# A decoder trunk on one core: output projection and feed-forward in one block, the norm's factor applied behind the gate and up products

## The chip, the cores and the metric

The kernel runs on one core of a Trainium2 chip. The metric is the device time of one execution in microseconds (us), the median of several runs. The core has five engines that run side by side, each with its own queue: TensorE (PE; its weight loads are shown apart as PEld), VectorE (DVE), ScalarE (ACT), GpSimd (POOL) and SyncE (SP), which here only issues DMAs. They wait for each other by semaphores that are written out by hand.

## The reference, cut to what matters

Two layers (one even, one odd) work on 1024 prompt tokens and 32 sample tokens, 1056 in all. Each layer is a mixer and a feed-forward part:

```python
def rmsnorm(x, g):
    xf = x.astype(f32)
    return xf * lax.rsqrt(jnp.mean(xf * xf, -1, keepdims=True) + EPS) * g

def swiglu(h, wg, wu, wd):
    return (jax.nn.silu(h @ wg) * (h @ wu)) @ wd

x = x + concat(mixer outputs) @ w_out        # 1024 x 1024
x = x + swiglu(rmsnorm(x, norm_ffn), w_gate, w_up, w_down)   # FF = 2816
```

The factor `rsqrt(mean(x*x) + EPS)` is one number for each token; the gain `g` is one number for each of the 1024 features.

## The kernel before, in words

**Layout.** Activations lie transposed: a tile of 128 partitions (features) by 1056 columns (tokens), eight such tiles for the 1024 features (KD = 8). `g.xt` is the residual stream x, `g.ht` a scratch of the same shape that holds the mixer's output at first, `g.hh` and `g.hl` the high and low halves of the right operand.

**Matrix products.** Every float32 product of these stages is made of three passes in the fp32r type: each operand is split in a high part (rounded by a copy on ACT) and a low part (the difference, a subtraction on DVE), and `split_passes` (L1709) issues high x high, high x low and low x high, each in three thirds of 352 columns. So one weight tile of 128 x 128 costs nine matmuls, and one output tile (eight weight tiles) 72.

**Output projection**, `stage_project_out` (L1510), a block of its own. ACT and DVE split the mixer's output (L1560 to L1563, L1584). For each of the eight output tiles m, SP loads the weights (L1528), ACT and DVE split them (L1558, L1579), PE makes 72 matmuls into PSUM banks 0 to 2 or 4 to 6 (m even or odd), and DVE adds them into x (L1596). ACT squares the new x (L1610) and DVE adds up the squares (L1618), one tile behind.

**Norm**, `split_norm` (L1623), which is the first part of the block of `stage_ffn` (L1718). Its steps follow one another: PE sums the squares over the partitions with nine small products against a column of ones (L1662); DVE scales and adds EPS (L1678), ACT takes the root (L1651), DVE the reciprocal (L1682), all on a tile of 128 x 9; DVE makes nine diagonal tiles (L1686), and PE multiplies them by ones (L1667), which gives the factor replicated over all partitions in PSUM, 128 x 1056. Then DVE multiplies each of the eight tiles of x by gain and factor (L1694), ACT rounds it into `g.hh` (L1656), and DVE and POOL take the low halves in turn (L1643).

**Feed-forward**, the rest of `stage_ffn`. FF = 2816 is 22 hidden tiles f, two for each of 11 chunks. For each hidden tile PE makes the gate product G(f) in banks 0 to 2 and the up product U(f) in banks 3 to 5 (72 matmuls each), and then half of the down product of the chunk before (four output tiles, 72 matmuls in all, banks 0 to 2 and 3 to 5 in turn). ACT applies Silu to the gate (L1874), DVE multiplies it with the up product (L1917), ACT and DVE split the result (L1878, L1922), and DVE adds each down product into x (L1929). Meanwhile SP loads the next weight tiles, ACT rounds them (L1868) and DVE takes their low parts (L1908). Three chunks stand unrolled ahead of a hardware loop and two behind it.

**Order.** Nothing plans the order: it is that of each engine's own program. On DVE a half chunk reads: low part of the down weights, low part of the next gate weights, join (L1917), low part of the next up weights, low part of the hidden tile, four additions into x. On ACT: round the down weights, Silu, round the next gate and up weights, round the hidden tile. PE waits for the split weights, and for a bank to be read before it writes there again; in the lines quoted here `silu` and `joined` are the counts of Silus and joins done:

```python
                                if c == 1 and half == 1:
                                    pe.wait_ge(added, 3 + n)
                                else:
                                    pe.wait_ge((silu, joined)[n], 2 * c + half)
```

Of the kernel before, what the change touches and what calls it, by code (L numbers as in the profile page):

```python
# [23 lines left out]
P = 128  # L24
D = 1024
# [131 lines left out]
def build_program(nc, ins, outs, const_dram, place, kept):  # L157
    with ExitStack() as whole:
# [37 lines left out]
        with ExitStack() as even:  # L196
# [1313 lines left out]
def stage_project_out(g, weight, tag, reload):  # L1510

    nc = g.nc
    x_in, made, added = (g.sem(f"{tag}_{n}") for n in ("stream", "made", "added"))
    w_in, w_rounded, w_split = g.slot_sems(f"{tag}_weights", 2), g.sem(f"{tag}_w_rounded"), g.sem(f"{tag}_w_split")
    rounded, split = g.sem(f"{tag}_rounded"), g.sem(f"{tag}_split")
    square, add_square, _ = sum_squares(g, f"{tag}n", g.ht[:, SQUARES, :], g.ht[:, TOTAL, :])
    with ExitStack() as st:
        w = g.room(st, f"{tag}_w", [P, 2, KD * P])
        wh = g.room(st, f"{tag}_wh", [P, 2, KD * P], F32R)
        wl = g.room(st, f"{tag}_wl", [P, 2, KD * P], F32R)  # L1520
        block = st.enter_context(nc.Block())

        @block.sync
        def _(sp):
            for m in range(KD):
                if m >= 2:
                    sp.wait_ge(w_split, m - 1)
                sp.dma_start(w[:, m % 2, :].rearrange("p (k n) -> p k n", k=KD),  # L1528
                             weight[:, m * P:(m + 1) * P].rearrange("(k p) n -> p k n", p=P)
                             ).then_inc(w_in[m % 2], 16)  # L1530

        @block.gpsimd
        def _(pool):
            if reload:
                for k in range(KD):
                    pool.dma_start(g.xt[:, k, :], g.xt_spill[:, k, :]).then_inc(x_in, 16)

        @block.tensor
        def _(pe):
            for m in range(KD):  # L1540
                pe.wait_ge(w_split, m + 1)
                if m >= 2:
                    pe.wait_ge(added, m - 1)
                for k in range(KD):
                    if m == 0:
                        pe.wait_ge(split, k + 1)
                    cols = slice(k * P, (k + 1) * P)
                    last = split_passes(g, pe, 4 * (m % 2), wh[:, m % 2, cols], wl[:, m % 2, cols], g.hh[:, k, :],
                                        g.hl[:, k, :], k == 0, k == KD - 1)
                last.then_inc(made, 1)  # L1550

        @block.scalar
        def _(act):
            def high(m):
                act.wait_ge(w_in[m % 2], 16 * (m // 2 + 1))
                if m >= 2:
                    act.wait_ge(made, m - 1)
                act.copy(wh[:, m % 2, :], w[:, m % 2, :]).then_inc(w_rounded, 1)  # L1558

            act.copy(g.hh[:, 0, :], g.ht[:, 0, :]).then_inc(rounded, 1)  # L1560
            high(0)
            for k in range(1, KD):
                act.copy(g.hh[:, k, :], g.ht[:, k, :]).then_inc(rounded, 1)  # L1563
            for m in range(1, KD):
                high(m)
                if m >= 2:
                    if m == 2:
                        act.wait_ge(split, KD)
                    act.wait_ge(added, m - 1)
                    square(act, m - 2)  # L1570
            for m in range(KD - 2, KD):
                act.wait_ge(added, m + 1)
                square(act, m)

        @block.vector
        def _(dve):
            def low(m):
                dve.wait_ge(w_rounded, m + 1)
                dve.tensor_tensor(wl[:, m % 2, :], w[:, m % 2, :], wh[:, m % 2, :].bitcast(F32), ALU.subtract  # L1579
                                  ).then_inc(w_split, 1)  # L1580

            for k in range(KD):
                dve.wait_ge(rounded, k + 1)
                dve.tensor_tensor(g.hl[:, k, :], g.ht[:, k, :], g.hh[:, k, :].bitcast(F32), ALU.subtract  # L1584
                                  ).then_inc(split, 1)
                if k == 0:
                    low(0)
            low(1)
            for m in range(KD):
                dve.wait_ge(made, m + 1)  # L1590
                if reload and m == 0:
                    dve.wait_ge(x_in, 16 * KD)
                if m + 2 < KD:
                    low(m + 2)
                xv = g.xt[:, m, :].rearrange("p (c n) -> p c n", c=3)
                dve.tensor_tensor(xv, g.ps[:, 4 * (m % 2):4 * (m % 2) + 3, 0:THIRD], xv, ALU.add).then_inc(added, 1)  # L1596
                if m >= 1:
                    add_square(dve, m - 1)
            add_square(dve, KD - 1)


# [116 lines left out]
def stage_ffn(g, layer):  # L1718

# [9 lines left out]
    KINDS = "GUD"  # L1729
    raw_in = dict(zip(KINDS, g.slot_sems(f"{tag}_raw_in", 3)))  # L1730
# [3 lines left out]
    silu, joined, hid_high, hid_low, added = (g.sem(f"{tag}_{n}") for n in  # L1734
                                              ("silu", "joined", "hid_high", "hid_low", "added"))
    source = {"G": g.ins["w_gate"][layer], "U": g.ins["w_up"][layer], "D": g.ins["w_down"][layer]}

    with ExitStack() as st:
        inverse = g.room(st, f"{tag}_inverse", [P, TILES])
        n_scalar, n_tensor, n_vector, n_gpsimd, wait_normed = split_norm(  # L1740
            g, 2 + layer, f"{tag}n", g.ht[:, SQUARES, :], g.ht[:, TOTAL, :], inverse[:, :], squares_done=True)
# [26 lines left out]
        def _(sp):  # L1768
# [19 lines left out]
            def chunk(c, par):  # L1788
                if at(c, 0):
                    load("G", 0, True)  # L1790
# [15 lines left out]

            chunks(sp.Fori, chunk)

        @block.tensor
        def _(pe):  # L1810
            def hidden(kind, f, first=False):
# [9 lines left out]
            def down(c, par, half, tail=False):  # L1821
# [4 lines left out]
                for m in range(4):  # L1826
                    if tail or m >= 2:
                        pe.wait_ge(added, 8 * c - 9 + 4 * half + m)
                    else:
                        pe.wait_ge((silu, joined)[m], 2 * c + half + 1)  # L1830
# [984 lines left out]
```

## Time and profile before

| | |
|---|---|
| median of three runs | 3229.15 us (3225.47 to 3239.33) |
| the profiled execution's own time | 3233.79 us |
| its span (first to last instruction) | 3231.7 us |
| PE busy | 2905.4 us (90% of the span) |
| DVE, ACT, POOL busy | 1493.0, 730.5, 314.2 us |
| mean granted PE clock | 0.928 |
| output projection of layer 0 | about 959 to 1061 us of the span |
| feed-forward of layer 0 | about 1061 to 1859 us |
| output projection and feed-forward of layer 1 | about 2316 to 3214 us |

The profile shows one execution. Busy times overlap between engines, and matmuls are pipelined, so that the records of neighbouring matmuls overlap too. A granted clock of 1.00 is 2.4 GHz, 0.50 is 1.2 GHz. In a timeline row the first number is the start in us, the second the length of the merged stretch, and the bracket at its end the idle time before it and what ended it.

### The profile page before, as it was taken

What the parts mean: (1) busy time and instruction counts of PE and PEld (TensorE: products, weight loads), DVE (VectorE), ACT (ScalarE), POOL (GpSimd) and SP (SyncE); (2) the same over time, 40 slices, a digit from 0 to 9 for tenths busy, and PEclk for the clock granted to TensorE, in tenths of its full rate; (3) what the DMA queues carried; (4) which work ended last, traced back from release to release, by engine and by line L of the source; (5) the groups of instructions that cost most, each with busy time, mean ns of one, the idle gap of its engine ahead of it and who ended that gap; (6) DMA issues with size and microseconds to landing.
All of it is one profiled execution on the core that took longest, in us unless ns stands there. A gap on an engine that the chain in (4) does not pass through costs nothing. (4 is left out here: it accounts for less than half of the span.)

```text
span 3231.7 us, 38976 instructions
## 1 busy us (share of the span) xinstructions
PE 2905.4 (90%) x16549; PEld 2663.2 (82%) x16549; DVE 1493.0 (46%) x2021; ACT 730.5 (23%) x1166; POOL 314.2 (10%) x287
## 2 busy tenths in 40 slices
PE   8889996638879899999999979958799999999998
PEld 7757775627539899999999979836599999999997
DVE  4789994678313433322332345248423332332333
ACT  3533330235321311111111032132312111111110
POOL 1022222512130100000000010015001000000000
PEclk9989998858989899999999989957699999999999
DMA  5022223143132121121121021010202111112111
GB/s 163 7 87 90 95 73 125 48 141 106 48 123 66 46 59 40 40 60 40 40 59 40 14 44 47 22 33 1 62 21 65 40 53 46 40 43 57 40 40 67
DMA packets 210737, 188.18 MB, mean 58 GB/s; under 512 B 22843, under 2 KB 164415, under 8 KB 210425
## 3 DMA queue, kind: packets, MB, share of 16 engines
q1 hardware_dynamic: 204033, 164.36, 16.9%
q0 software_dynamic: 6528, 21.23, 2.2%
q8 instruction: 139, 2.28, 0.3%
q14 instruction: 37, 0.30, 0.0%
HBM read 152.25 MB, written 33.50 MB: 57 GB/s over the span
## 5 line engine op out<-in xcount | busy, mean ns | idle before, releaser
L1929 DVE TENSOR_TENSOR xt<-ps,xt 128x1056 f32<-128x1056 f32 x176 | 221.0, 1256 | 205.7 <-PE ps L1713 205.7
L1713 PE MATMUL ps<-ffn_high,f_whG 128*128 128x352 f32 x1056 | 230.0, 326 | 13.2 <-DVE ffn_low L1643 7.8
L1713 PE MATMUL ps<-f_hidh,f_whD 128*128 128x352 f32 x1056 | 229.6, 326 | 9.9 <-DVE f_wlD L1908 9.9
L1713 PE MATMUL ps<-ffn_low,f_whG 128*128 128x352 f32 x1056 | 229.1, 325 | 0.0
L1713 PE MATMUL ps<-f_hidh,f_wlD 128*128 128x352 f32 x1056 | 228.9, 325 | 0.0
L1713 PE MATMUL ps<-ffn_low,f_whU 128*128 128x352 f32 x1056 | 228.7, 324 | 0.0
L1713 PE MATMUL ps<-f_hidl,f_whD 128*128 128x352 f32 x1056 | 228.4, 324 | 0.0
L1713 PE MATMUL ps<-ffn_high,f_whU 128*128 128x352 f32 x1056 | 227.8, 324 | 0.0
L1713 PE MATMUL ps<-ffn_high,f_wlG 128*128 128x352 f32 x1056 | 227.6, 324 | 0.0
L1713 PE MATMUL ps<-ffn_high,f_wlU 128*128 128x352 f32 x1056 | 226.6, 323 | 0.0
L728 PE MATMUL ps<-pe_wh,even_high 128*128 128x512 f32 (+1 forms) x504 | 200.2, 397 | 13.3 <-POOL pe_wl L760 13.3
L730 PE MATMUL ps<-pe_wh,even_low 128*128 128x512 f32 (+1 forms) x504 | 198.9, 395 | 0.0
L729 PE MATMUL ps<-pe_wl,even_high 128*128 128x512 f32 (+1 forms) x504 | 198.3, 394 | 0.0
L1713 PEld LDWEIGHTS ps<-ffn_high,f_whG 128*128 128x128 f32 x1056 | 180.3, 190 | 15.5 <-issue 13.2
L1713 PEld LDWEIGHTS ps<-f_hidh,f_whD 128*128 128x128 f32 x1056 | 181.2, 190 | 11.1 <-DVE f_wlD L1908 11.1
L1713 PEld LDWEIGHTS ps<-f_hidh,f_wlD 128*128 128x128 f32 x1056 | 181.9, 189 | 0.0
L1713 PEld LDWEIGHTS ps<-ffn_low,f_whG 128*128 128x128 f32 x1056 | 181.1, 189 | 0.0
L1713 PEld LDWEIGHTS ps<-ffn_high,f_wlG 128*128 128x128 f32 x1056 | 180.9, 189 | 0.0
L1713 PEld LDWEIGHTS ps<-f_hidl,f_whD 128*128 128x128 f32 x1056 | 180.7, 189 | 0.0
L1713 PEld LDWEIGHTS ps<-ffn_high,f_wlU 128*128 128x128 f32 x1056 | 180.5, 189 | 0.0
L1713 PEld LDWEIGHTS ps<-ffn_low,f_whU 128*128 128x128 f32 x1056 | 179.6, 187 | 0.0
L1713 PEld LDWEIGHTS ps<-ffn_high,f_whU 128*128 128x128 f32 x1056 | 179.4, 188 | 0.0
(538 smaller groups left out, 4837.5 us busy)
## 6 DMA issues: line engine op xcount, KB each, us to landing
pe_w<-in_w_in_even_dram SPq DMA_DIRECT2D x7, 2048.0 KB, 8.3
proj<-pe_out SPq DMA_DIRECT2D x56, 256.0 KB, 2.0
ht_even<-in_w_gate_dram SPq DMA_DIRECT2D x22, 512.0 KB, 5.1
ht_even<-in_w_up_dram SPq DMA_DIRECT2D x22, 512.0 KB, 6.3
ht_even<-in_w_down_dram SPq DMA_DIRECT2D x22, 512.0 KB, 3.9
ht_odd<-in_w_gate_dram SPq DMA_DIRECT2D x22, 512.0 KB, 5.1
ht_odd<-in_w_up_dram SPq DMA_DIRECT2D x22, 512.0 KB, 6.3
ht_odd<-in_w_down_dram SPq DMA_DIRECT2D x22, 512.0 KB, 3.9
```

Of the source, the lines that this page charges most:

```text
L728: pe.matmul(to, high, wh[:, m % 2, k, :], start=(k == 0), stop=False)
L729: pe.matmul(to, high, wl[:, m % 2, k, :], start=False, stop=False)
L730: last = pe.matmul(to, low, wh[:, m % 2, k, :], start=False, stop=(k == KD - 1))
L1713: last = pe.matmul(g.ps[0:out_rows, b0 + c, 0:THIRD], lhs, rhs[:, c * THIRD:(c + 1) * THIRD], start=(first and n == 0), stop=(final and n ...
L1929: dve.tensor_tensor(xv, g.ps[:, 3 * (m % 2):3 * (m % 2) + 3, 0:THIRD], xv, ALU.add).then_inc(added, 1)
```

## The change

The two blocks of a layer become one, `stage_mix_out`, and `split_norm` is no longer used there (the odd layer's input stage still has it).

- PE goes from the last output tile of the projection straight to G(0). Of the last output tile, each of the eight weight tiles counts up a semaphore `used`, and as soon as a tile of `g.hh` and `g.hl` has been used for the last time, ACT and DVE overwrite it with the high and low parts of gain times x (`high_x`, `low_x`), with no factor in it.
- The squares now lie in two slots (there were four). Behind G(0), PE multiplies the summed squares by an all-ones 128 x 128 tile: three float32 matmuls, two of 512 columns and one of 32 (`replicate`), into banks 6, 7 and the free end of bank 2. DVE takes mean and EPS from PSUM into an SBUF tile of 128 x 1056 in three pieces, ACT takes the root of that tile, DVE its reciprocal.
- In each of the 22 hidden tiles, DVE multiplies the gate product by the factor (`scale`, PSUM to SBUF), ACT applies Silu to that SBUF tile in place, and DVE multiplies the result once more by the factor (`regate`), so that the join with the unscaled up product is right. PE's wait for banks 0 to 2 is now for `scaled`.
- DVE's order in a half chunk is now: low part of the down weights, `scale`, `regate`, low part of the next gate weights, join, and so on. ACT's Silu waits for `scaled` instead of the gate product.
- POOL has no part in the low halves any more. The projection's split weights lie in the room of the hidden tiles, and the first gate, up and down weights are loaded, and the gate and up weights split, while the projection still runs.

```diff
 def build_program(nc, ins, outs, const_dram, place, kept):
...
-            stage_project_out(g, ins["w_out_even"][0], "oe", reload=True)
-            stage_ffn(g, 0)
+            stage_mix_out(g, ins["w_out_even"][0], 0, reload=True)
...
-            stage_project_out(g, ins["w_out_odd"][0], "oo", reload=False)
-            stage_ffn(g, 1)
+            stage_mix_out(g, ins["w_out_odd"][0], 1, reload=False)
...
-def stage_ffn(g, layer):
+def stage_mix_out(g, weight, layer, reload):
...
+    total, inverse = g.ht[:, 7, :], g.ht[:, 5, :]
+    square, add_square, squares_added = sum_squares(g, f"{tag}n", g.ht[:, 3:5, :], total)
...
+        out_wh, out_wl = (x[:, :, :, :].rearrange("p a b n -> p (a b n)")[:, 0:2 * KD * P]
+                          .rearrange("p (s n) -> p s n", s=2) for x in (hidh, hidl))
         gate, prod = g.ht[:, 3, :], g.ht[:, 4, :]
+        spreads = ((0, 6, 0, 512), (512, 7, 0, 512), (SEQ, 2, THIRD, NS))
+        gain = g.gain[:, 2 + layer, :]
...
         def _(pe):
+            def mix(m):
+                pe.wait_ge(w_split, m + 1)
+                if m >= 2:
+                    pe.wait_ge(joined_x, m - 1)
+                for k in range(KD):
+                    if m == 0:
+                        pe.wait_ge(mix_split, k + 1)
+                    cols = slice(k * P, (k + 1) * P)
+                    last = split_passes(g, pe, 4 * (m % 2), out_wh[:, m % 2, cols], out_wl[:, m % 2, cols],
+                                        g.hh[:, k, :], g.hl[:, k, :], k == 0, k == KD - 1)
+                    if m == KD - 1:
+                        last.then_inc(used, 1)
+                if m < KD - 1:
+                    last.then_inc(made_out, 1)
+
+            def replicate():
+
+                pe.wait_ge(squares_added, KD)
+                for t0, bank, to, n in spreads:
+                    last = pe.matmul(g.ps[:, bank, to:to + n], g.c("ones"), total[:, t0:t0 + n], start=True, stop=True)
+                last.then_inc(spread_out, 1)
+
             def hidden(kind, f, first=False):
                 pe.wait_ge(split[kind], f + 1)
                 for k in range(KD):
                     if first:
-                        wait_normed(pe, k)
+                        pe.wait_ge(x_split, k + 1)
...
-                                    pe.wait_ge((silu, joined)[n], 2 * c + half)
+                                    pe.wait_ge((scaled, joined)[n], 2 * c + half)
+                            else:
+                                pe.wait_ge(joined_x, KD - 1 + n)
...
                         hidden(kind, 2 * c + half, first=at(c, 0) and half == 0 and n == 0)
+                        if at(c, 0) and half == 0 and n == 0:
+                            replicate()
...
         def _(act):
+            def high_x(k):
+                act.wait_ge(used, k + 1)
+                act.wait_ge(joined_x, k + 1)
+                act.activation(g.hh[:, k, :], g.xt[:, k, :], ACT.Copy, scale=gain[:, k:k + 1]).then_inc(x_rounded, 1)
...
-            def activate(f, first=False):
-                act.wait_ge(made["G"], f + 1)
-                if not first:
-                    act.wait_ge(joined, f)
-                act.activation(thirds(gate), g.ps[:, 0:3, 0:THIRD], ACT.Silu).then_inc(silu, 1)
+            def activate(f):
+                act.wait_ge(scaled, f + 1)
+                act.activation(gate, gate, ACT.Silu).then_inc(silu, 1)
...
             high("G", 0, True)
             high("U", 0, True)
-            n_scalar[1](act)
+            for k in range(KD):
+                if k in (0, KD - 1):
+                    act.wait_ge(joined_x, KD - 1 if k == 0 else KD)
+                    square(act, KD - 2 if k == 0 else KD - 1)
+                high_x(k)
+            act.wait_ge(mean_ready, 1)
+            act.activation(inverse, inverse, ACT.Sqrt).then_inc(root_ready, 1)
             chunks(act.Fori, chunk)
...
         def _(dve):
...
+            def low_x(k):
+                dve.wait_ge(x_rounded, k + 1)
+                dve.scalar_tensor_tensor(out=g.hl[:, k, :], in0=g.xt[:, k, :], scalar=gain[:, k:k + 1],
+                                         in1=g.hh[:, k, :].bitcast(F32), op0=ALU.mult, op1=ALU.subtract
+                                         ).then_inc(x_split, 1)
...
+            def scale(f):
+                dve.wait_ge(made["G"], f + 1)
+                dve.tensor_tensor(thirds(gate), g.ps[:, 0:3, 0:THIRD], thirds(inverse), ALU.mult).then_inc(scaled, 1)
+
+            def regate(f):
+                dve.wait_ge(silu, f + 1)
+                dve.tensor_tensor(gate, gate, inverse, ALU.mult).then_inc(gated, 1)
+
             def join(f, first=False):
-                dve.wait_ge(silu, f + 1)
+                dve.wait_ge(gated, f + 1)
...
                 if not at(c, 0):
                     low("D", 2 * c - 2)
+                scale(2 * c)
+                regate(2 * c)
                 low("G", 2 * c + 1)
                 join(2 * c, first=at(c, 0))
...
-            n_vector[0](dve)
...
+            for m in range(KD - 1):
+                join_x(m)
+                if m >= 1:
+                    add_square(dve, m - 1)
             low("G", 0)
             low("U", 0)
-            n_vector[1](dve)
+            add_square(dve, KD - 2)
+            for k in range(KD - 1):
+                low_x(k)
+            join_x(KD - 1)
+            low_x(KD - 1)
+            add_square(dve, KD - 1)
+            dve.wait_ge(spread_out, 1)
+            for t0, bank, to, n in spreads:
+                last = dve.tensor_scalar(inverse[:, t0:t0 + n], g.ps[:, bank, to:to + n], 1.0 / D, EPS, ALU.mult, ALU.add)
+            last.then_inc(mean_ready, 1)
+            dve.wait_ge(root_ready, 1)
+            dve.reciprocal(inverse, inverse).then_inc(inverse_ready, 1)
+            dve.wait_ge(inverse_ready, 1)
             chunks(dve.Fori, chunk)
```

`join_x(m)` is the former addition into x (L1590 to L1596) under another name; for the last tile it waits for `used` to reach eight.

## Rows read from the trace of the kernel before

**Rows 1.** The page, part 1: busy time of each engine.

```profile
PE 2905.4 (90%) x16549; PEld 2663.2 (82%) x16549; DVE 1493.0 (46%) x2021; ACT 730.5 (23%) x1166; POOL 314.2 (10%) x287
```

**Rows 2.** Busy time by stretch: length, PE, PEld, DVE, ACT, POOL, PEclk, DMA share, GB/s.

```profile
1300.00:1500.00 200.00, 199.16 (x1236) 198.87 (x1235) 58.53 (x49) 28.85 (x28) 0.00 (x0) 1.00 0.17 48
1050.00:1060.00 10.00, 10.00 (x64) 10.00 (x63) 1.40 (x2) 1.09 (x1) 0.00 (x0) 1.00 0.00 0
1100.00:1110.00 10.00, 10.00 (x64) 10.00 (x63) 3.65 (x3) 2.13 (x2) 0.00 (x0) 1.00 0.18 53
```

**Rows 3.** Timeline of PE between the projection and U(0), layer 0.

```profile
1064.74 3.74 PE L1662 MATMUL ps<-cst,ht_even 128*128 128x1 f32 x18 [4.14 <-PEq L1517]
1069.60 4.35 PE L1667 MATMUL ps<-ht_even,cst 128*128 128x128 f32 x18 [1.12 <-DVE ht_even L1686]
1077.84 1.22 PE L1713 MATMUL ps<-ffn_high,f_whG 128*128 128x352 f32 x3 [3.90 <-DVE ffn_low L1643]
...
1082.01 0.65 PE L1713 MATMUL ps<-ffn_high,f_wlG 128*128 128x352 f32 x3
1082.49 0.65 PE L1713 MATMUL ps<-ffn_high,f_whG 128*128 128x352 f32 x3
```

**Rows 4.** Timeline of DVE, layer 0: last two additions of the projection, first join.

```profile
1048.98 1.26 DVE L1596 TENSOR_TENSOR xt<-ps,xt 128x1056 f32<-128x1056 f32 x1 [6.88 <-PE ps L1713]
...
1060.64 1.26 DVE L1596 TENSOR_TENSOR xt<-ps,xt 128x1056 f32<-128x1056 f32 x1 [9.24 <-PE ps L1713]
...
1104.56 1.26 DVE L1917 TENSOR_TENSOR ht_even<-ps,ht_even 128x1056 f32<-128x1056 f32 x1 [8.45 <-PE ps L1713]
```

**Rows 5.** Timeline of DVE, layer 1: last addition of the projection, first join.

```profile
2418.40 1.26 DVE L1596 TENSOR_TENSOR xt<-ps,xt 128x1056 f32<-128x1056 f32 x1 [9.24 <-PE ps L1713]
...
2461.28 1.26 DVE L1917 TENSOR_TENSOR ht_odd<-ps,ht_odd 128x1056 f32<-128x1056 f32 x1 [8.45 <-PE ps L1713]
```

**Rows 6.** Timeline of PE in the sample attention: a run of float32 matmuls.

```profile
939.72 16.47 PE L1449 MATMUL ps<-pages,as_kt 128*128 128x512 f32 x38
```

**Rows 7.** Groups by line and form: xcount | busy us, mean ns | idle before, releaser.

```profile
L590 DVE COPY fr_scale<-ps 128x512 f32<-128x512 f32 x2 | 1.3, 686 | 4.1 <-PE ps L395 4.1
L1694 DVE SCALAR_TENSOR_TENSOR ht_even<-xt,gain,ps 128x1056 f32<-128x1056 f32 x8 | 10.1, 1308 | 0.6 <-PE ps L1667 0.6
L1908 DVE TENSOR_TENSOR f_wlG<-ht_even,f_whG 128x1024 fp32r<-128x1024 f32 x22 | 26.9, 1225 | 229.2 <-ACT f_whG L1868 229.2
L1656 ACT CAST ffn_high<-ht_even 128x1056 fp32r<-128x1056 f32 x8 | 8.6, 1079 | 7.8 <-DVE ht_even L1694 7.3
```

**Rows 8.** Timeline of ACT, layer 0: the table load ahead of the first Silu.

```profile
1088.54 1.28 ACT L1874 ACT_TABLE_LOAD   x1
```

**Rows 9.** Reciprocals, by line: duration in ns as min/median/max.

```profile
L1345 DVE RECIPROCAL at_stat<-at_stat x32: 144/159/164, 747.0 to 840.2; 128x1 f32<-128x1 f32 x32
...
L1682 DVE RECIPROCAL f_inverse<-f_inverse x2: 215/216/217, 1069.0 to 2426.3; 128x9 f32<-128x9 f32 x2
...
L2775 DVE RECIPROCAL sd_rs<-sd_rs x1: 267/267/267, 2303.1 to 2303.1; 128x18 f32<-128x18 f32 x1
...
L1055 DVE RECIPROCAL rt_ms<-rt_ms x1: 379/379/379, 667.8 to 667.8; 128x36 f32<-128x36 f32 x1
```

**Rows 10.** Who waited for whom, layer 0's feed-forward (1110 to 1858 us): total, times, longest.

```profile
PE ps L1713 <- DVE f_wlD L1908: 5.0, 2, 2.5
```

**Rows 11.** Busy time by stretch, columns as in rows 2: six us from each such stall's end.

```profile
1828.00:1834.00 6.00, 5.16 (x22) 5.16 (x23) 1.19 (x2) 0.00 (x0) 0.00 (x0) 0.72 0.28 87
1844.00:1850.00 6.00, 5.22 (x23) 5.23 (x24) 1.35 (x2) 0.00 (x0) 0.00 (x0) 0.72 0.00 0
3186.00:3192.00 6.00, 6.00 (x27) 6.00 (x28) 1.26 (x1) 0.00 (x0) 0.00 (x0) 0.72 0.25 87
3202.00:3208.00 6.00, 6.00 (x38) 6.00 (x39) 1.26 (x1) 0.00 (x0) 0.00 (x0) 1.00 0.01 3
```

More of the change, by code:

```diff
@@ L1507, in _ @@
                                     [list(turned_out.ap[0]), [P + NT, H], [H * NT, NB], [1, NT]]))
[L1510 to L1599, printed above, removed]
@@ L1729, in stage_ffn @@
     KINDS = "GUD"
+    x_in, made_out, joined_x = (g.sem(f"{tag}_{n}") for n in ("stream", "made_out", "added_out"))
+    w_in, w_rounded, w_split = g.slot_sems(f"{tag}_weights", 2), g.sem(f"{tag}_w_rounded"), g.sem(f"{tag}_w_split")
+    mix_rounded, mix_split, used = g.sem(f"{tag}_mix_rounded"), g.sem(f"{tag}_mix_split"), g.sem(f"{tag}_used")
+    x_rounded, x_split = g.sem(f"{tag}_x_rounded"), g.sem(f"{tag}_x_split")
+    spread_out, mean_ready, root_ready, inverse_ready = (g.sem(f"{tag}_{n}") for n in
+                                                         ("spread", "mean", "root", "inverse_ready"))
     raw_in = dict(zip(KINDS, g.slot_sems(f"{tag}_raw_in", 3)))
@@ L1805, in chunk, with _ @@
                     load("U", 2 * c + 2)
-            chunks(sp.Fori, chunk)
+            for m in range(KD):
+                if m >= 2:
+                    sp.wait_ge(w_split, m - 1)
+                sp.dma_start(w[:, m % 2, :].rearrange("p (k n) -> p k n", k=KD),
+                             weight[:, m * P:(m + 1) * P].rearrange("(k p) n -> p k n", p=P)
+                             ).then_inc(w_in[m % 2], 16)
+            chunks(sp.Fori, chunk)
+        @block.gpsimd
+        def _(pool):
+            if reload:
+                for k in range(KD):
+                    pool.dma_start(g.xt[:, k, :], g.xt_spill[:, k, :]).then_inc(x_in, 16)
         @block.tensor
         def _(pe):
+            def mix(m):
+                pe.wait_ge(w_split, m + 1)
+                if m >= 2:
+                    pe.wait_ge(joined_x, m - 1)
[14 more added lines that the diff above has]
+                last.then_inc(spread_out, 1)
             def hidden(kind, f, first=False):
@@ L1829, in down @@
                     else:
[L1830 removed]
+                        pe.wait_ge((scaled, joined)[m], 2 * c + half + 1)
                     for k in range(2):
@@ L1883, in chunk @@
                     high("D", 2 * c - 2, first=at(c, 1))
-                activate(2 * c, first=at(c, 0))
+                activate(2 * c)
                 high("G", 2 * c + 1)
@@ L1905, in _, with low_out, join_x @@
         def _(dve):
+            def low_out(m):
+                dve.wait_ge(w_rounded, m + 1)
+                dve.tensor_tensor(out_wl[:, m % 2, :], w[:, m % 2, :], out_wh[:, m % 2, :].bitcast(F32), ALU.subtract
+                                  ).then_inc(w_split, 1)
+            def join_x(m):
+                if m < KD - 1:
+                    dve.wait_ge(made_out, m + 1)
+                else:
+                    dve.wait_ge(used, KD)
+                if reload and m == 0:
+                    dve.wait_ge(x_in, 16 * KD)
+                if m + 2 < KD:
+                    low_out(m + 2)
+                xv = thirds(g.xt[:, m, :])
+                dve.tensor_tensor(xv, g.ps[:, 4 * (m % 2):4 * (m % 2) + 3, 0:THIRD], xv, ALU.add).then_inc(joined_x, 1)
+            def low_x(k):
[3 more added lines that the diff above has]
+                                         ).then_inc(x_split, 1)
             def low(kind, x):
@@ L1942, in chunk @@
                     low("D", 2 * c - 1)
+                scale(2 * c + 1)
+                regate(2 * c + 1)
                 if not final:
```

40 lines of the change are left out of this document (30 added, 10 removed).

## The prediction, made before the changed kernel was run

> **What bounds the kernel now.** I read the page's busy times first: PE is busy for nine tenths of the span, DVE for under half, ACT for a quarter [rows 1]. So only what moves PE's work, or the gaps in it, moves the end. Next the busy times by stretch: inside the feed-forward PE has no gaps to speak of (199.16 of 200 us) at a granted clock of 1.00 [rows 2]. There nothing can be won without fewer matmuls, and the change takes none away. Then the places where PE does stop. The largest in these two stages is the way from the projection to the feed-forward. After the last projection product PE starts the small sums 4.14 us late, for a new block begins; sums and replication take 3.74 and 4.35 us of short products in which the array does little, with 1.12 us between; then it waits 3.90 us for the first split tile; and the gate product starts at 1.22 us for three matmuls against 0.65 later on [rows 3], at half clock. The whole way, from the last addition of the projection, which starts as its last product ends, to the first join, which starts as U(0) ends, takes 1104.56 - 1060.64 = 43.92 us in layer 0 [rows 4] and 2461.28 - 2418.40 = 42.88 us in layer 1 [rows 5]. Of this only G(0) and U(0) are needed.
>
> **A unit.** Three matmuls of 352 columns follow the last three after 1082.49 - 1082.01 = 0.485 us [rows 3] (0.48 as printed; several such steps give 0.485), so a weight tile costs 1.455 us and a product of 72 matmuls 24 x 0.485 = 11.65 us. Times below are us after the last projection product ended.
>
> **The change, part by part.**
>
> *Block boundary, sums, replication and scaling are gone from between the products.* PE can begin G(0) at 0 if the split tiles are there. That has to be followed on DVE. Its addition of output tile 6 starts as the last output tile does, at -11.65 [rows 4]. From there it does that addition, a sum of squares, two weight splits, another sum, seven `low_x` and the last addition: six instructions at up to 1.26 and seven at up to 1.31 us, the price of the like instruction that reads PSUM [rows 4, 7]. That is 16.7 us, so the last addition ends at 5.1. ACT then squares (1.1) and rounds (1.1) tile 7 [rows 7], DVE takes its low half (1.3) and the last sum (1.25): the eighth split tile stands at 8.6, the sum at 9.9. PE wants the eighth tile at 7 x 1.455 = 10.2 and the sum at 11.65. Slack 1.6 and 1.8 us, so I cost `high_x` and `low_x` at nothing; the cover is G(0) itself, and if it were short, each us late would be a us on PE, in each layer. Tiles 0 to 6 are overwritten behind the counts of `used`, one every 1.455 us, and rounding (1.1) keeps up; what sets their time is DVE, and tile 4, the first one made after 0, is ready near 1.3 and wanted at 5.8. POOL's share of the low halves is gone from the path.
>
> *Weights.* SP's queue now passes the first gate, up and down loads behind the eighth projection load, whose slot comes free as output tile 3 ends, four tiles or 46 us before 0; they only wait for the mixer's output to be split, which is older still. DMA share there is near zero [rows 2]. Nothing.
>
> *Replication.* Each float32 matmul shows as two records (the nine sums of L1662 are x18 [rows 3]). With 512 columns a record takes 16.47 / 38 = 0.43 us [rows 6], so two matmuls are 1.73 us, and I give 0.15 to the one of 32 columns: 1.9 us, on the path of PE. It ends at 13.55, and U(0) at 25.2.
>
> *The factor.* Behind the replication: mean and EPS in three pieces from PSUM, two at 0.69 [rows 7] and a short one, 1.5, to 15.0; root on ACT, 1.1 [rows 7], to 16.1. The table load for the root has stood before the wait, and the one for Silu (1.28 [rows 8]) fits while DVE takes the reciprocal. That reciprocal is the unknown: the trace has none beyond 36 columns. From 9 to 36 columns it grows by (379 - 216) / 27 = 6.04 ns a column [rows 9], so 1056 columns make 0.38 + 1020 x 6.04 ns = 6.5 us. The low end is the price of an ordinary instruction of that length, 1.3 us; the high end is twice the slope, 12.8 us, as nothing near this length is shown. I take 6.5: the slope is steady between the rows. It ends at 22.6.
>
> *The Trainium skill on this.* The page "VectorE: DVE Perf Modes", section "First, the fixed hardware budget", says that a reciprocal runs as an iterative divide with a repeat count of 8. If that meant eight cycles for each column at the 0.96 GHz of the quick reference of "Trainium Kernel Development and Optimization", an estimate from the pages would be 8.8 us, 2.3 more in each layer, and the result 3204.5; the slope in rows 9 speaks for less.
>
> *The first hidden tile.* PE reaches G(1) at 25.2. G(1) needs its weights split, and on DVE that split now stands behind `scale` and `regate`. From 22.6: scale 1.26 (23.9), Silu 1.1 (25.0), regate 1.26 (26.2), low part of the gate weights 1.23 (27.5) [rows 4, 7]. ACT's rounding of those weights (1.1) runs beside `regate`. So PE waits 2.3 us and G(1) starts at 27.5, not 25.2. Everything behind it has time: the join and the split of the up weights end near 30, wanted at 39.
>
> *The sum of this.* Layer 0: 43.9 - 27.5 = 16.4. Layer 1: 42.9 - 27.5 = 15.4. Together 31.8 us.
>
> *The clock.* A stall of 2.5 us [rows 10] already stands twice in each layer's last chunk, four in all. In the six us behind it the granted clock was 0.72 on average three times and 1.00 once [rows 11]. 0.72 over six us is 0.28 x 6 = 1.7 us of PE's time. The new stall is nearly as long, one for each layer, so I take off 2 x 0.75 x 1.7 = 2.5 us. Gain 29.3.
>
> *The steady part.* In each of the 44 hidden tiles DVE does two more instructions of 1.26 us and ACT none (Silu reads SBUF instead of PSUM). Queued behind them are the gate weights' split and, later, the join. `scale` starts when G ends; `regate` is done by 3.6, the split by 4.9 after G, and U takes 11.65: DVE is waiting for U again by then, as it is today (8.45 us idle before a join [rows 4]). PE waits for the gate weights only after U and the down product. Banks 0 to 2 come free at the same time as before. Cost nothing; the cover is some 6 us of DVE's idle time under U. SP's next gate load waits for the split and so starts about 2 us later, with over 10 us to spare.
>
> Against the profiled execution (3233.79) this makes 3204.5. That execution was 4.6 us above the median of the runs, 3229.15, so for the median I say **3199.9**.
>
> **Rivals.**
>
> *No stall at G(1).* A reciprocal at the low end would leave the whole chain done by 22.3, before U(0) ends at 25.2. Then 43.9 + 42.9 - 2 x 25.2 = 36.4 us are won and the clock stays: 3192.8. For it: every other long DVE instruction here costs near 1.2 ns a column. Against it: the slope of rows 9.
>
> *A dearer reciprocal.* At twice the slope the stall is 8.6 us, and the gain 31.8 - 12.6 - 3.4 (clock lost both times) = 15.8: 3213.4. For it only that no row is as long; from 9 columns down to 1 the slope is (216 - 159) / 8 = 7.1 ns [rows 9], not much more.
>
> *Slower.* The added DVE work disturbs PE in every hidden tile: 44 x 2.52 = 111 us of added instructions, half of them reading PSUM while PE writes there. If PE ran at half pace under them it would lose 55 us against 29 won: 3229 + 26 = 3255. It decides from 29.3 / 88 = 0.33 us lost for each added instruction. Against it: in ten us with 3.65 us of DVE work PE issues 64 matmuls, as in ten us with 1.40 [rows 2].
>
> *The change does not take the way out.* If the split tiles came late (DVE's list longer than I count, or the squares in two slots holding ACT up), G(0) would start in pieces. Eight us late in each layer would leave 13 us, 3216. The slack of 1.6 us speaks against it, thin as it is.
>
> **How the numbers follow.** The forecast (3195 to 3206, with the reciprocal between 5.5 and 9 us and the clock lost never or twice) gets 0.76, no stall 0.07, a dearer reciprocal 0.08, late tiles 0.05, slower 0.04. The range of 3190 to 3211 holds the forecast, the case without stall and the cheaper half of the dear reciprocals, and some 2 us at each end for the scatter of a median (the runs before lie 14 us apart). A measurement of this kernel can tell about 0.5%, 16 us, from no change: below 3213 counts as faster. Forecast, no stall and most of the dear reciprocals lie there, 0.91; the same 0.05; slower 0.04.
>
> **What would show it.** Right: no idle time on PE between the last projection product and G(0); two pairs of long float32 records behind G(0); a reciprocal near 6.5 us; one gap of 2 to 2.5 us before G(1) that ends on the split of the gate weights; 27.5 us from the last projection product to G(1). In the steady part the join still waits for PE, and PE is busy for over 99%. Wrong: gaps inside G(0) (late tiles), a reciprocal of 1 or 12 us, more than 0.485 us for three matmuls while `scale` runs, or the gate weights' split as a releaser of PE in later chunks.

## The result, and the profile after

| | before | changed |
|---|---|---|
| median | 3231.94 us (8 runs, 3225.47 to 3239.33) | 3213.47 us (8 runs, 3205.95 to 3218.39) |
| profiled execution's own time, span | 3233.79, 3231.7 us | 3209.71, 3207.9 us |
| DVE busy | 1493.0 us | 1602.9 us |

The ratio is 0.9939 (95% interval 0.9928 to 0.9950): faster by 16 to 23 us, 18.5 by the medians. Forecast were 29.3 and a time of 3199.9, in a range of 3190 to 3211. The sign was right, the size was not. Of the 13.6 us between the forecast time and the measured one, 10.8 are missing gain; the other 2.8 are the kernel before, whose median was 3229.15 us in the first three runs and 3231.94 in all eight.

The page's first part and a stretch inside the first feed-forward, which answer to [rows 1, 2] (columns of the second as there):

```profile
PE 2901.5 (90%) x16489; PEld 2659.8 (83%) x16489; DVE 1602.9 (50%) x2083; ACT 734.6 (23%) x1166; POOL 293.4 (9%) x279
```

```profile
1300.00:1500.00 200.00, 198.98 (x1230) 198.69 (x1229) 78.11 (x65) 29.23 (x29) 0.00 (x0) 1.00 0.14 41
```

PE is as busy as before, at the same granted clock, but in the same 200 us it issues 1230 matmuls and not 1236. That is where the largest part of the missing gain is; more below.

**The way from the projection to the feed-forward.** The timeline of PE in layer 0, which answers to [rows 3]:

```profile
1056.65 0.65 PE L1619 MATMUL ps<-ffn_high,f_hidl 128*128 128x352 f32 x3
1057.14 0.65 PE L1619 MATMUL ps<-ffn_high,f_whG 128*128 128x352 f32 x3
...
1068.31 0.65 PE L1619 MATMUL ps<-ffn_high,f_wlG 128*128 128x352 f32 x3
1068.80 2.02 PE L1754 MATMUL ps<-ht_even,cst 128*128 128x512 f32 x6
1070.65 0.73 PE L1619 MATMUL ps<-ffn_high,f_whU 128*128 128x352 f32 x3
...
1085.13 0.72 PE L1619 MATMUL ps<-ffn_high,f_whG 128*128 128x352 f32 x3 [2.59 <-DVE f_wlG L1903]
```

The first row is the end of the last projection product (its split weights now lie in `f_hidh` and `f_hidl`); G(0) follows it with no gap. The float32 product takes 1068.80 to 1070.65, then U(0). The one gap, 2.59 us, ends on the low part of the next gate weights. The timeline of DVE over the same time says why:

```profile
1045.68 1.26 DVE L1893 TENSOR_TENSOR xt<-ps,xt 128x1056 f32<-128x1056 f32 x1 [6.88 <-PE ps L1619]
...
1060.07 1.25 DVE L1893 TENSOR_TENSOR xt<-ps,xt 128x1056 f32<-128x1056 f32 x1
1063.54 1.32 DVE L1897 SCALAR_TENSOR_TENSOR ffn_low<-xt,gain,ffn_high 128x1056 fp32r<-128x1056 f32 x1 [2.22 <-ACT ffn_high L1820]
1064.78 1.25 DVE L1524 TENSOR_TENSOR ht_even<-ht_even 128x1056 f32<-128x1056 f32 x1
1070.85 1.39 DVE L1980 TENSOR_SCALAR ht_even<-ps 128x512 f32<-128x512 f32 x3 [4.82 <-PE ps L1754]
1073.39 6.75 DVE L1983 RECIPROCAL ht_even<-ht_even 128x1056 f32<-128x1056 f32 x1 [1.16 <-ACT ht_even L1871]
1080.18 1.26 DVE L1908 TENSOR_TENSOR ht_even<-ps,ht_even 128x1056 f32<-128x1056 f32 x1
1082.59 1.26 DVE L1912 TENSOR_TENSOR ht_even<-ht_even 128x1056 f32<-128x1056 f32 x1 [1.15 <-ACT ht_even L1830]
1083.77 1.22 DVE L1903 TENSOR_TENSOR f_wlG<-ht_even,f_whG 128x1024 fp32r<-128x1024 f32 x1
```

The last output tile starts at 1045.68, and the last product ends 11.65 us later, at 1057.33. From there the eighth split tile stands at 7.5 us and the last sum at 8.7 (forecast 8.6 and 9.9, wanted at 10.2 and 11.65). Reciprocal, `scale`, Silu, `regate` and the split form one chain, and G(1) starts at 27.8 (forecast 27.5).

The way is measured below to the join of hidden tile 1, behind U(1), so that the loss of clock behind the stall is in it. The rows that give it, for layer 0 and layer 1 (in layer 1 of the changed kernel, output tile 7 starts at 2394.52): first the kernel before, then the changed one:

```profile
1127.79 1.26 DVE L1917 TENSOR_TENSOR ht_even<-ps,ht_even 128x1056 f32<-128x1056 f32 x1 [8.44 <-PE ps L1713]
2484.52 1.26 DVE L1917 TENSOR_TENSOR ht_odd<-ps,ht_odd 128x1056 f32<-128x1056 f32 x1 [8.44 <-PE ps L1713]
```

```profile
1110.30 1.26 DVE L1920 TENSOR_TENSOR ht_even<-ps,ht_even 128x1056 f32<-128x1056 f32 x1 [6.90 <-issue]
2394.52 1.26 DVE L1893 TENSOR_TENSOR xt<-ps,xt 128x1056 f32<-128x1056 f32 x1 [6.88 <-PE ps L1619]
2459.13 1.26 DVE L1920 TENSOR_TENSOR ht_odd<-ps,ht_odd 128x1056 f32<-128x1056 f32 x1 [6.90 <-issue]
```

That is 67.2 and 66.1 us before, 52.95 and 52.95 after.

The busy times of the six us behind that gap, one row for each layer, with the clock as in [rows 11]:

```profile
1085.00:1091.00 6.00, 5.87 (x27) 5.90 (x28) 3.55 (x3) 1.07 (x1) 0.00 (x0) 0.72 0.60 175
2434.00:2440.00 6.00, 6.00 (x28) 6.00 (x29) 3.38 (x3) 1.08 (x1) 0.00 (x0) 0.72 0.60 175
```

The granted clock was at half for part of it in both layers: 0.28 x 6 = 1.7 us each. The four stalls in the last chunks, which [rows 11] shows for the kernel before, are there after the change as well, each of 2.48 us:

```profile
1814.00:1820.00 6.00, 5.51 (x34) 5.51 (x35) 1.69 (x2) 0.00 (x0) 0.00 (x0) 1.00 0.27 87
1828.00:1834.00 6.00, 5.11 (x22) 5.11 (x23) 1.25 (x2) 0.00 (x0) 0.00 (x0) 0.72 0.01 3
3162.00:3168.00 6.00, 5.98 (x37) 5.98 (x38) 1.26 (x1) 0.00 (x0) 0.00 (x0) 1.00 0.27 90
3176.00:3182.00 6.00, 5.58 (x34) 5.58 (x35) 1.63 (x2) 0.00 (x0) 0.00 (x0) 1.00 0.00 0
```

Here the clock fell once in four, before the change three times in four. The stalls are as long as before, so that difference is luck of the two profiled executions.

**The steady part.** Two joins that follow one another in the first feed-forward, from the timelines of DVE, first the kernel before, then the changed one:

```profile
1185.86 1.26 DVE L1917 TENSOR_TENSOR ht_even<-ps,ht_even 128x1056 f32<-128x1056 f32 x1 [8.44 <-PE ps L1713]
1220.67 1.26 DVE L1917 TENSOR_TENSOR ht_even<-ps,ht_even 128x1056 f32<-128x1056 f32 x1 [8.44 <-PE ps L1713]
```

```profile
1203.52 1.26 DVE L1920 TENSOR_TENSOR ht_even<-ps,ht_even 128x1056 f32<-128x1056 f32 x1 [6.90 <-issue]
1238.48 1.26 DVE L1920 TENSOR_TENSOR ht_even<-ps,ht_even 128x1056 f32<-128x1056 f32 x1 [6.90 <-issue]
```

From join to join, three products of 72 matmuls, it takes 34.81 us before and 34.96 after, and this repeats to 0.01 us in most steps. DVE is idle for 6.9 us ahead of the join in either layer, so its queue has not closed up. (The profile names no releaser for that wait; but the join at 1238.48 starts 0.25 us after PE began the product behind U, at 1238.23, so it still waits for PE.) PE itself is slower, by 0.7 ns for each matmul (161.9 for 161.2). With about 40 such steps in the two feed-forwards this is 40 x 0.147 = 5.9 us. Nothing in the forecast had it.

### The profile page after: what moved, and what is told of

It is laid out like the page before. It is cut to its first block and busy times, and to the rows that moved or that the text cites. A ratio compares the mean times of both kernels' runs of the same rounds, so it can differ in the third digit from the quotient of the medians.

```text
span 3207.9 us, 38868 instructions
## 1 busy us (share of the span) xinstructions
PE 2901.5 (90%) x16489; PEld 2659.8 (83%) x16489; DVE 1602.9 (50%) x2083; ACT 734.6 (23%) x1166; POOL 293.4 (9%) x279
```

## The experiments

All times "from the last projection product" are read as above: the start of the addition of output tile 6 plus 11.65 us.

**The pace: addresses or DVE's added work?** The change takes away a tile of 128 x 9 (36 bytes a partition) that lay ahead of the block's other tiles, and adds DVE work under PE. (It also lays the projection's raw weights, two slots of 4096 bytes a partition, ahead of the split ones; e1_offset leaves them there.) Three kernels tell these apart.

```diff
 # e1_offset, on the changed kernel
+        g.room(st, f"{tag}_pad", [P, TILES])
         w = g.room(st, f"{tag}_w", [P, 2, KD * P])
```

> The changed kernel with one unused tile of 128 x 9 (36 bytes a partition) laid out ahead of its own tiles, as the norm's small tile was in the kernel before. The whole computation is done. Theory A (the steady part grew from 34.81 to 34.96 us from join to join because the tiles that PE reads lie at other addresses): 34.81 here, so some 6 us less over the two feed-forwards. Theory B (it grew because DVE now does two more instructions in each hidden tile): 34.96 as in the changed kernel.

```diff
 # e2_before_aligned, on the kernel before: stage_ffn
-        inverse = g.room(st, f"{tag}_inverse", [P, TILES])
...
         hidl = g.room(st, f"{tag}_hidl", [P, 2, 2, T], F32R)
+        inverse = g.room(st, f"{tag}_inverse", [P, TILES])
```

> The kernel before with the small tile of 128 x 9 laid out behind the feed-forward's other tiles instead of ahead of them; nothing else is touched. Theory A (addresses): 34.96 us from join to join instead of 34.81. Theory B (added DVE work): 34.81 as before.

```diff
 # e3_no_scale, on the changed kernel
-                scale(2 * c)
-                regate(2 * c)
...
-                scale(2 * c + 1)
-                regate(2 * c + 1)
...
-                act.activation(gate, gate, ACT.Silu).then_inc(silu, 1)
+                act.activation(thirds(gate), g.ps[:, 0:3, 0:THIRD], ACT.Silu).then_inc(silu, 1)
```

The waits for `scaled` on PE and for `gated` in the join are for `silu` there, as in the kernel before.

> The changed kernel without scale and regate in the hidden tiles: ACT applies Silu straight from PSUM as before, so the factor of the norm is left out of the result; it is still computed. Theory A (addresses): 34.96 us from join to join, as in the changed kernel. Theory B (added DVE work): back to 34.81. Under both the first gate split still stands behind the reciprocal: ready near 24.1 us after the last projection product instead of 27.8, so before U(0) ends at 25.3, and no stall at G(1).

Two joins in a row from the timelines of DVE of e1_offset, of e2_before_aligned and of e3_no_scale, in this order:

```profile
1201.48 1.26 DVE L1921 TENSOR_TENSOR ht_even<-ps,ht_even 128x1056 f32<-128x1056 f32 x1 [6.88 <-issue]
1236.30 1.26 DVE L1921 TENSOR_TENSOR ht_even<-ps,ht_even 128x1056 f32<-128x1056 f32 x1 [6.87 <-issue]
```

```profile
1182.08 1.26 DVE L1917 TENSOR_TENSOR ht_even<-ps,ht_even 128x1056 f32<-128x1056 f32 x1 [8.47 <-PE ps L1713]
1217.04 1.26 DVE L1917 TENSOR_TENSOR ht_even<-ps,ht_even 128x1056 f32<-128x1056 f32 x1 [8.46 <-PE ps L1713]
```

```profile
1197.59 1.26 DVE L1922 TENSOR_TENSOR ht_even<-ps,ht_even 128x1056 f32<-128x1056 f32 x1 [8.47 <-PE ps L1619]
1232.55 1.26 DVE L1922 TENSOR_TENSOR ht_even<-ps,ht_even 128x1056 f32<-128x1056 f32 x1 [8.46 <-PE ps L1619]
```

34.81, 34.96 and 34.96. The unused 36 bytes bring the old pace back under all of DVE's new work, so the raw weights ahead of them are not the cause either; moving the small tile away gives the kernel before the slow pace with none of it; and taking DVE's work out of the changed kernel does not help the pace. All three verdicts go to the addresses. Single times: 3200.76, 3235.62 and 3197.09 us beside 3229.89 for the kernel before on that chip. The first and the third lie some 7 us lower than the traces explain from 3213.47 (one run each, against eight that spread over 12 us), so the pace is read from the profiles.

e3_no_scale also had no stall at G(1), as both theories said: the join of hidden tile 1 starts 48.6 us after the last projection product, where the changed kernel has 52.95.

**The stall at G(1).** e4_early_split does the split of the second gate tile where DVE waits for the root:

```diff
 # ACT
-                high("G", 2 * c + 1)
+                if not at(c, 0):
+                    high("G", 2 * c + 1)
...
+            high("G", 1)
             act.wait_ge(mean_ready, 1)
...
 # DVE
-                low("G", 2 * c + 1)
+                if not at(c, 0):
+                    low("G", 2 * c + 1)
...
             last.then_inc(mean_ready, 1)
+            low("G", 1)
             dve.wait_ge(root_ready, 1)
```

> The changed kernel with the second gate tile's weights rounded on ACT ahead of the root and their low part taken on DVE between the mean and the reciprocal, where DVE waits for ACT. My theory (the stall of 2.59 us at G(1) is the queue position of that split behind scale and regate, and the half clock behind the stall follows from it): the split is ready near 17 us, scale is done near 24.2, U(0) ends at 25.3, no gap at G(1), no half clock behind it: 2.6 + 1.7 us in each layer, 8.6 in all, against the changed kernel. Rival (the stall moves: scale comes late because the split delays the reciprocal, or the clock falls anyway): a gap of over 1 us before G(1) that ends on scale, or a fall of the clock without one, and 0 to 4 us in all.

From its timeline of DVE, and the busy times behind the place where the stall was:

```profile
1071.14 1.39 DVE L1983 TENSOR_SCALAR ht_even<-ps 128x512 f32<-128x512 f32 x3 [4.83 <-PE ps L1754]
1072.45 1.22 DVE L1905 TENSOR_TENSOR f_wlG<-ht_even,f_whG 128x1024 fp32r<-128x1024 f32 x1
1073.68 6.75 DVE L1987 RECIPROCAL ht_even<-ht_even 128x1056 f32<-128x1056 f32 x1
1080.47 1.26 DVE L1910 TENSOR_TENSOR ht_even<-ps,ht_even 128x1056 f32<-128x1056 f32 x1
```

```profile
1078.00:1084.00 6.00, 6.00 (x39) 6.00 (x39) 4.81 (x3) 2.14 (x2) 0.00 (x0) 1.00 0.00 0
```

The split fits into the root's time, PE has no gap, and the clock stays at 1.00. The join of tile 1 starts at 48.6 in both layers instead of 52.95: 8.7 us in all, where my theory had 8.6. Measured: 3201.81 us (four runs, 3198.45 to 3205.56), ratio to the kernel before 0.9909 (0.9893 to 0.9926) against 0.9939 of the changed kernel. The intervals lie 0.0002 apart; the 8.7 us are read from the trace.

**What covers the chain.** e9_sum_first puts the all-ones product ahead of G(0):

```diff
-        spreads = ((0, 6, 0, 512), (512, 7, 0, 512), (SEQ, 2, THIRD, NS))
+        spreads = ((0, 6, 0, 512), (512, 7, 0, 512), (SEQ, 3, THIRD, NS))
...
                                 pe.wait_ge(joined_x, KD - 1 + n)
+                                if n == 1:
+                                    pe.wait_ge(mean_ready, 1)
...
-                        hidden(kind, 2 * c + half, first=at(c, 0) and half == 0 and n == 0)
                         if at(c, 0) and half == 0 and n == 0:
                             replicate()
+                        hidden(kind, 2 * c + half, first=at(c, 0) and half == 0 and n == 0)
```

The added wait keeps U(0) out of bank 3 until DVE has read the sum there.

> The changed kernel with the all-ones product ahead of G(0) instead of behind it, so that PE waits for the last sum of squares with nothing under it (the sample's 32 columns go to the free end of bank 3 for that); the whole computation is done. My theory (the gain is G(0) and U(0) covering the chain of the norm): the last sum stands 8.7 us after the last projection product, the product ends at 10.7, G(0) starts at half clock and ends near 24, U(0) at 35.7, no stall at G(1); the join of hidden tile 1 starts 59 us after the last projection product instead of 52.95, so some 6 us in each layer, 12 in all, slower than the changed kernel. Rival (the gain is the block boundary and the serial steps on the small tile, and it does not matter where the sums stand): within 3 us of the changed kernel.

Its timeline of PE:

```profile
1062.39 4.02 PE L1754 MATMUL ps<-ht_even,cst 128*128 128x512 f32 x6 [8.86 <-DVE ht_even L1524]
1066.22 1.23 PE L1619 MATMUL ps<-ffn_high,f_whG 128*128 128x352 f32 x3
```

PE waits 8.86 us for the last sum, and then the float32 product takes 4.02 us instead of 2.02, for the clock is at half (1.23 us for three matmuls of G(0) again, as in [rows 3]). At the added wait PE has no idle time. The join of tile 1 starts at 60.6 and 60.4, against 59 expected and 52.95 in the changed kernel: 15.1 us in all, 3 more than forecast, for I had not doubled the float32 product. Measured 3225.28 us (10 runs), ratio 0.9984 (0.9974 to 0.9994). So with the blocks merged and the factor moved, but with nothing under the sums, 6.0 us by the medians are left of the 18.5: two thirds of the gain are gone. The rival, that the block boundary and the small serial steps were the cost and the place of the sums is of no account, falls.

**Both remedies in one kernel.** e5_early_offset has the early split and the 36 bytes.

> The early split of the second gate tile and the unused 36 bytes a partition in one kernel; the whole computation is done. If the two effects are independent: 34.81 us from join to join, no stall at G(1), and against the changed kernel 8.7 us (early split, by its trace) plus 5.9 us (40 steps of 0.147 us) = 14.6 us less, so near 3199 where the changed kernel has 3213. Rival: the stall's end or the loop edges take back part of it, and it is no better than the early split alone.

34.81 us from join to join, the join of tile 1 at 48.4, 3195.10 us (five runs, 3190.42 to 3198.31), ratio 0.9888 (0.9871 to 0.9905). Expected was 3199; it is better by 4 us, and 3199 lies inside the interval of the ratio. In the traces the two effects add.

**Which shift?** Five kernels with the early split and another width of the unused tile; 36 bytes is the one above.

```diff
-        g.room(st, f"{tag}_pad", [P, TILES])
+        g.room(st, f"{tag}_pad", [P, 1])     # 4 bytes; 8, 16, 24, 32 columns for 32, 64, 96, 128 bytes
```

> The same with 4 bytes a partition in place of 36. If any shift off the aligned place gives the faster pace: 34.81 us from join to join. If it is the size of 36 bytes: 34.96 or another value.

> The same with 32 bytes a partition. If what counts is that 36 is no multiple of 32 or 64: 34.96 us from join to join here. If any shift counts: 34.81.

> The kernel with the early split and 64 bytes a partition ahead of the other tiles. 4 and 32 bytes gave the same pace of every product (34.993 us from join to join), 36 bytes another (34.813). If places are rounded up to 32 bytes, so that 4 and 32 are one shift and 36 and 64 another: 34.81 here. If 36 bytes is a place of its own: something else.

> The same with 96 bytes a partition. If the pace goes by the place within 64 bytes: 34.99 as with 32. If within 128 bytes or more: a value not seen so far.

> The same with 128 bytes a partition. If the pace goes by the place within 128 bytes: 34.96 as in the changed kernel without a shift. If within more: another value. If shifts of 64 bytes and up are all as good: 34.81.

From join to join, and the mean start-to-start of matmuls by product, worked out from their starts in the traces (first feed-forward, 1150 to 1780 us):

| bytes ahead | join to join, us | high x G high, ns | low x G high, ns | high x G low, ns | hidden high x D high, ns |
|---|---|---|---|---|---|
| 0 (changed kernel) | 34.96 | 162.4 | 161.5 | 161.5 | 162.5 |
| 4 | 34.99 | 161.3 | 162.9 | 162.1 | 162.2 |
| 32 | 34.99 | 161.4 | 162.9 | 162.1 | 162.2 |
| 36 | 34.81 | 161.1 | 161.7 | 159.9 | 161.0 |
| 64 | 34.81 | 161.1 | 161.7 | 159.9 | 161.0 |
| 96 | 34.68 | 160.0 | 160.0 | 160.0 | 162.2 |
| 128 | 34.90 | 162.2 | 161.2 | 161.6 | 161.2 |

4 and 32 bytes are one place, 36 and 64 another, product by product: the places behave as if rounded up to 32 bytes. The kernel before and e2_before_aligned show the rows of 36 and of 0, within 0.2 ns. Of the expectations, 4 bytes gave neither 34.81 nor 34.96 but "another value", 34.99; 32 bytes gave neither of the two that were expected; 64 bytes gave the 34.81 that follows if places are rounded up. With 96 bytes the pace is not that of 32, with 128 not that of 0, so neither 64 nor 128 bytes is a period, and these shifts show no other. The joins of the kernel with 96 bytes:

```profile
1193.45 1.26 DVE L1923 TENSOR_TENSOR ht_even<-ps,ht_even 128x1056 f32<-128x1056 f32 x1 [6.77 <-issue]
1228.13 1.26 DVE L1923 TENSOR_TENSOR ht_even<-ps,ht_even 128x1056 f32<-128x1056 f32 x1 [6.77 <-issue]
```

There all three gate products and all three up products run at 160.0 ns, and only the down products stay above 161.

**The best of them, timed.** e12_best is the kernel with the early split and 96 bytes.

> The early split with 96 bytes a partition ahead, timed. From the traces: the changed kernel (3213.5) less 8.7 us for the early split and 40 x (34.96 - 34.68) = 11.2 us for the pace, near 3193.5; against the kernel with 36 bytes 40 x 0.133 = 5.3 us less. Rival (the pace of one profiled run is no property of the kernel and moves from run to run): the median lies at that of the kernel with 36 bytes, 3195, or above, and the profile shows another period.

3187.94 us (four runs, 3187.11 to 3188.25), ratio to the kernel before 0.9859 (0.9843 to 0.9876): 45.5 us below it, and 25.5 below the changed kernel by the medians (other chip). It shows the same 34.68:

```profile
1195.50 1.26 DVE L1923 TENSOR_TENSOR ht_even<-ps,ht_even 128x1056 f32<-128x1056 f32 x1 [6.77 <-issue]
1230.18 1.26 DVE L1923 TENSOR_TENSOR ht_even<-ps,ht_even 128x1056 f32<-128x1056 f32 x1 [6.77 <-issue]
```

The pace of a place came out the same in every profile of it and on every chip tried, so it is a property of the kernel. The time lies 5.6 us under the 3193.5 expected. About half of that is gain that the expectation left out: the two projections run at the better pace too (78.4 us from the first addition to the last product's end, where the changed kernel takes 79.2), and the join of tile 1 comes at 47.96 where e4_early_split has 48.61, which makes 1.6 + 1.3 = 2.9 us. The rest goes with the changed kernel's median, of which more below.

## Why the prediction missed

- **Split tiles and sums in time: right.** 7.5 and 8.7 us against 8.6 and 9.9; no gap inside G(0). e9_sum_first shows what this cover is worth, 15 us in the two layers.
- **Weights early, replication 1.9 us: right.** 1.85, six records, at full clock.
- **The reciprocal: right.** 6.75 us against 6.5. The slope of rows 9, from tiles of at most 36 columns, held up to 1056: (6753 - 379) / 1020 = 6.25 ns a column. The estimate of 8.8 us made from the Trainium skill's page "VectorE: DVE Perf Modes", section "First, the fixed hardware budget", is not borne out; at the 0.96 GHz of the Trainium skill's "Trainium Kernel Development and Optimization", quick reference, the measured slope would be six cycles a column, an estimate, not eight.
- **The stall: right in place and nearly in size.** 2.59 against 2.3 us, on the releaser named. G(1) at 27.8 against 27.5.
- **The clock: right mechanism, a little small.** Half clock behind the stall in both layers, 3.4 us where I took 2.5, and in both again in e1_offset. No stall, no loss (e4_early_split).
- **The way as a whole.** Last projection product to the join of tile 1: 67.2 and 66.1 us before, 52.95 and 52.95 after, so 27.4 us against the forecast 29.3. The later start of G(1) is 0.6 us of the difference, the clock 0.9.
- **The steady part, "Cost nothing": wrong.** This is the step that failed. I looked for what the added instructions would do to DVE's queue and to PE under them, and both were in fact free (e3_no_scale has the same 34.96 without them). What I did not look at was the line of the diff that drops the small tile ahead of the others and so moves the split weights and the hidden tiles that PE reads. It costs 5.9 us, and e1_offset and e2_before_aligned show it in both directions. The rival "slower" priced a slower PE, but by the wrong cause, and the sign of being wrong that I gave, more than 0.485 us for three matmuls, was too coarse: the two paces are 0.4835 and 0.4856 (34.81 and 34.96 us for 72 such steps).
- **The output stage at the end: not in the forecast.** The change does not touch its code, yet from the last addition into x to the end it takes 19.4 to 19.9 us in the eleven profiles of the changed kernel and of those that keep `scale` and `regate`, against 17.8 in the kernel before and in e2_before_aligned (18.3 in e3_no_scale). In the changed kernel DVE's copies wait 2.6 us in all for output DMAs that it waits 0.4 us for in the kernel before. That is 1.75 us more; why is open.

27.4 - 5.9 - 1.75 = 19.7 us is what these leave, and the medians say 18.5, with 16 to 23 as the interval. The two profiled spans differ by 23.8, and their traces say where (us):

| stretch | before | changed | difference |
|---|---|---|---|
| start to the first addition of the projection, layer 0 | 981.5 | 978.2 | -3.3 |
| the two projections, from there to the last product's end | 158.4 | 158.4 | 0.0 |
| on to the join of tile 1, both layers | 133.3 | 105.9 | -27.4 |
| join of tile 1 to that of tile 21, both layers | 1374.5 | 1379.0 | +4.5 |
| on to the last addition into x, both layers | 85.2 | 82.3 | -2.9 |
| on to the first addition of the projection of layer 1 | 481.0 | 484.6 | +3.7 |
| last addition into x, layer 1, to the end | 17.80 | 19.55 | +1.75 |

The fourth row has less than the pace makes of it because of one step: two steps in each layer are 1.1 to 1.5 us longer than the rest, before and after, but in layer 1 of the changed kernel one of them is not (34.96 us). The fifth is mostly the clock behind the stalls of the last chunks, lost three times before and once after. The first and the sixth row are stages that the change does not touch; over all fourteen profiles the first goes from 972.9 to 981.5 us and the sixth from 480.5 to 487.4. Together these four make the profiled pair look some 4 us better than what repeats: luck.

Without the 5.9 us the median would lie near 3207.6, inside the range. The measured median is itself unsure by about the 2.5 us that it lies outside: the eight runs form two groups, 3206 to 3210 and 3216 to 3218, and the variants timed several times (e4_early_split, e9_sum_first, e5_early_offset), by their ratios to the kernel before and what their traces differ in, put the changed kernel at 3210 to 3212 (for e4_early_split 0.9909 x 3231.94 + 8.7 = 3211.2). The scatter of the untouched stages is wide enough to part such groups; with one trace of the eight runs it is not shown that it did. Inside or outside the range, about a third of the forecast gain is missing, and the pace is the largest part of that.

## What to carry to other kernels

When a norm's factor is one number for each token, it can be applied behind the products, and the chain that makes it then costs only what sticks out from under the first of them; look for the instruction queued behind that chain, here the next weights' split, which was worth 8.7 us, clock included. In a kernel bound by TensorE, a diff that adds or drops a small buffer moves everything laid out behind it: compare the pace of the steady part before and after, and try a few shifts. Here 96 unused bytes a partition were worth 11 us in the steady part and about 14 with the projections and the first tiles (by the medians of e4_early_split and e12_best, 13.9).

## What the runs showed of the hardware

- **TensorE's pace depends on where its operands lie.** The same instructions at granted clock 1.00 take 159.9 to 163.1 ns each, by product, as the weights and hidden tiles are shifted by 0 to 128 bytes a partition; from join to join that is 34.68 to 34.99 us, 0.9%. The table above has four of the nine products; the 163.1 is low x U high with 4 and 32 bytes. A shift moves all of the block's own tiles but not `g.hh`, `g.hl`, x or the raw gate, up and down weights, so what counts is either a place itself or a distance between two; which, and for which operand, stays open.
- **A long reciprocal on DVE** takes 6.75 us for 1056 columns, 5.4 times a multiplication of the same tile (1.26 us).
- **Half clock doubles a float32 product too:** 4.02 us at half clock against 2.02 for the same six records.
- **A stall of about 2.5 us costs the clock in some cases and not in others.** In the two profiles before and after it came in six of ten cases: three of four at the ends of the layers before, one of four there after, and both at G(1) after. Over all fourteen profiles there are 61 such stalls of 2.4 to 2.7 us in the feed-forwards, and the six us behind them show a granted clock of 0.72 to 0.76 for 35 and of 1.00 for 26; the four at G(1), in the changed kernel and in e1_offset, are all among the 35. At 0.72, a loss is 0.28 x 6 = 1.7 us of granted clock.
